# FFN input products by seven block products for eight, in a streaming encoder step on one Trainium2 core

## The reference

```python
D_MODEL, SEQ, DEC_SEQ, D_FF = 1024, 512, 32, 2816

def swiglu(h, w_in, w_out):
    gate, up = jnp.split(h @ w_in, 2, axis=-1)
    return (jax.nn.silu(gate) * up) @ w_out

def encoder_layer(x, l):                     # shortened
    x = x + 0.5 * swiglu(rms_norm(x, ffn1_norm[l]), ffn1_w_in[l], ffn1_w_out[l])
    x = x + mixer(rms_norm(x, mix_norm[l]))
    x = x + 0.5 * swiglu(rms_norm(x, ffn2_norm[l]), ffn2_w_in[l], ffn2_w_out[l])
    return x
```

## Time and profile before

| | us |
|---|---|
| median of 3 runs | 2440.68 |
| lowest and highest | 2438.52 and 2443.16 |
| profiled execution, own time | 2437.53 |
| its span, first to last instruction | 2435.7 |
| TensorE busy | 2394.6 |
| VectorE busy | 1091.7 |
| ScalarE busy | 786.6 |
| GpSimd busy | 375.9 |

### The profile page before, as it was taken

One profiled execution on the slowest core, in us unless ns is written; L12 is line 12 of the kernel. 1 busy time (PEld: TensorE's weight loads), 2 busy tenths in 40 slices (PEclk: granted clock), 3 DMA queues, 4 the chain that ended last, 5 costly groups with the idle time before them and its releaser, 6 DMA issues.

```text
span 2435.7 us, 45344 instructions
## 1 busy us (share of the span) xinstructions
PE 2394.6 (98%) x19160; PEld 2344.4 (96%) x19160; DVE 1091.7 (45%) x1405; ACT 786.6 (32%) x1006; POOL 375.9 (15%) x324
## 2 busy tenths in 40 slices
PE   7999999999999999999999999999999999999998
PEld 7999999988989999999999999999999899999998
DVE  5333332556574333322433332488655654333322
ACT  4333322333323222222322222345345543222222
POOL 2101000000142111000111100143033531011000
PEclk9999999999999999999999999999999999999999
DMA  3223223322202222222222222323200012222221
GB/s 127 91 86 99 82 79 103 101 89 83 68 21 93 87 86 86 82 96 84 95 94 86 86 78 96 98 70 87 71 29 1 10 44 87 87 95 92 83 92 54
DMA packets 191213, 193.66 MB, mean 80 GB/s; under 512 B 4811, under 2 KB 188495, under 8 KB 191082
## 3 DMA queue, kind: packets, MB, share of 16 engines
q1 hardware_dynamic: 178286, 181.64, 23.1%
q10 hardware_dynamic: 12162, 8.11, 1.2%
q0 software_dynamic: 640, 2.10, 0.3%
HBM read 185.73 MB, written 6.10 MB: 79 GB/s over the span
## 4 chain that ended last, share of the span: by engine, by line
PE 94%; DVE 4%; issue 1%; ACT 1%; POOL 0%; DMA 0%; ACTq 0%; DVEq 0%
PE ps L573 81%; PE ps L2522 1%; PE ps L2507 1%; PE ps L2653 1%; DVE wl L558 1%; PE ps L2495 1%; PE ps L1092 0%; PE ps L1560 0%; PE ps L1657 0%; PE ps L780 0%; PE ps L2547 0%; PE ps L2541 0%; PE ps L2553 0%; PE ps L2562 0%; PE ps L1708 0%
## 5 line engine op out<-in xcount | busy, mean ns | idle before, releaser
L573 PE MATMUL ps<-xh,wh 128*128 128x288 f32 x3776 | 780.6, 288 | 3.6 <-DVE wl L558 2.8
L573 PE MATMUL ps<-xl,wh 128*128 128x288 f32 x3776 | 778.4, 287 | 0.0
L573 PE MATMUL ps<-xh,wl 128*128 128x288 f32 x3776 | 775.3, 287 | 0.0
L558 DVE TENSOR_TENSOR wl<-raw,wh 128x2048 fp32r<-128x2048 f32 (+1 forms) x173 | 390.7, 2258 | 505.0 <-ACT wh L553 505.0
L573 PEld LDWEIGHTS ps<-xh,wh 128*128 128x128 f32 x3776 | 577.4, 188 | 16.2 <-issue 8.0
L573 PEld LDWEIGHTS ps<-xh,wl 128*128 128x128 f32 x3776 | 578.1, 188 | 0.0
L573 PEld LDWEIGHTS ps<-xl,wh 128*128 128x128 f32 x3776 | 576.2, 188 | 0.0
L553 ACT ACTIVATE wh<-raw 128x2048 fp32r<-128x2048 f32 (+1 forms) x173 | 323.3, 1869 | 324.7 <-PE ps L573 318.8
L573 PE MATMUL ps<-hl,wh 128*128 128x288 f32 (+1 forms) x1408 | 289.9, 287 | 0.0
L573 PE MATMUL ps<-hh,wl 128*128 128x288 f32 (+1 forms) x1408 | 288.7, 286 | 0.0
L573 PE MATMUL ps<-hh,wh 128*128 128x288 f32 (+1 forms) x1408 | 286.7, 285 | 0.0
(11 more groups left out here) (430 smaller groups left out, 2191.5 us busy)
## 6 DMA issues: line engine op xcount, KB each, us to landing
raw<-ffn_w_in SPq DMA_DIRECT2D x88, 1024.0 KB, 5.1
raw<-ffn_w_out SPq DMA_DIRECT2D x32, 1024.0 KB, 5.1
raw<-odd_w_in SPq DMA_DIRECT2D x16, 1024.0 KB, 5.6
raw<-even_w_in SPq DMA_DIRECT2D x14, 1024.0 KB, 5.0
...
raw<-even_w_out SPq DMA_DIRECT2D x4, 1024.0 KB, 5.3
raw<-odd_w_out SPq DMA_DIRECT2D x4, 1024.0 KB, 5.4
xnat<-x_prompt SPq DMA_DIRECT2D x2, 1024.0 KB, 8.5
```

Source lines behind the costliest of these rows:

```text
L558: nc.vector.tensor_tensor(wl[slot][:, 0:kt, :], raw[slot][:, 0:kt, :], wh[slot][:, 0:kt, :].bitcast(F32), ALU.subtract).then_inc(lo_done.s ...
L573: ins = nc.tensor.matmul(ps[:, 2 * pe_out + b, PCOLS[b]], w, r[:, rk, TOKENS[b]], start=first and a == 0, stop=last and a == 2)
```

## The change

The input matrices. Each FFN keeps three kinds of units:

- the first gate unit, whole as before (96 matmuls);
- the other three units of the first two pairs, "plain": the same 96 matmuls, but the weights split in four blocks of 4 k tiles x 128 columns;
- the 18 units of the other nine pairs, "seven": the unit's weights are seen as 2 x 2 blocks (column tile c by depth half h), the normalised activations as 2 x 2 blocks (depth half by token half of 272 columns, `TH`), and the 2 x 2 x 2 = 8 block products become 7, each 4 k tiles x 3 passes = 12 matmuls of 272 columns into one bank: 84 matmuls. Two products are added onto a bank that holds an earlier one.

For this the activations of an FFN are normalised in full (gain and `rstd`) into `bopf`, POOL forms four block differences of them, and all seven operands are split into high and low (`bop`, 14 blocks). Of each seven unit's weights POOL forms four sums of blocks (`weight_sums`); three of the seven weight operands are raw blocks. ACT and DVE split the seven operands into a ring of eight block entries, which lies in the old `wh` and `wl` buffers. The four output blocks (2 column tiles x 2 token halves) are put together from the banks by ACT (a copy, `m1c`) and DVE (`u2c`, `u3c` and the sums onto them). No `rstd` is needed behind a seven unit, since its input is normalised.

The output matrix. The three weight parts (`HID_PARTS`, 8, 8 and 6 hidden tiles) are no longer an inner loop: after pairs 0 to 3 come four output units over hidden tiles 0 to 7, after pairs 4 to 7 four over tiles 8 to 15, after pairs 8 to 10 four over 16 to 21. `hh` and `hl` shrink to 8 tiles, `x` is added to three times a tile. The matmuls stay 1056. All loops of the FFNs, and those of the mixers' output matrices, are unrolled.

The core of the diff, added lines:

```diff
+    S_ORDER = (6, 2, 3, 1, 4, 0, 5)
+    S_BANK = (0, 1, 2, 3, 0, 1, 2)
+    S_OPEN = (0, 1, 2, 3, 5)
+    S_ADDED = (4, 6)
...
+    def op_split_hi(act, u, i):
+        op, slot = u.op + i, u.raw % 2
+        if i == 0:
+            act.wait_ge(raw_loaded[slot].sem, raw_loaded[slot].at(8 * (u.raw - slot) + 16))
+        if u.kind == "seven" and i in (1, 2, 3, 6):
+            act.wait_ge(sum_made.sem, sum_made.at(4 * u.seven + {1: 2, 2: 2, 3: 3, 6: 4}[i]))
+        if op in op_first:
+            act.wait_ge(unit_done.sem, unit_done.at(op_first[op]))
+        elif op_prev[op] is not None:
+            act.wait_ge(op_used.sem, op_used.at(op_prev[op] + 1))
+        nc.scalar.activation(entry(op)[0][:, 0:block_nk(u, i), :], op_source(u, i), ACT.Copy).then_inc(op_hi.sem, 1)
+
+    def op_split_lo(dve, u, i):
+        op, nk = u.op + i, block_nk(u, i)
+        hi, lo = entry(op)
+        dve.wait_ge(op_hi.sem, op_hi.at(op + 1))
+        nc.vector.tensor_tensor(lo[:, 0:nk, :], op_source(u, i), hi[:, 0:nk, :].bitcast(F32), ALU.subtract).then_inc(op_lo.sem, 1)
+
...
+    def ffn_seven_pe(pe, u, n):
+        f, bank = u.f, 4 * u.s
+        before = ffns[f][u.at - 2]
+        if before.kind == "plain":
+            done = gate_scaled if u.s == 0 else h_made
+            pe.wait_ge(done.sem, done.at((2 * LEAD_PAIRS if u.s == 0 else 2 * FJ) * f + 2 * LEAD_PAIRS))
+        elif before.kind == "out":
+            pe.wait_ge(x_part.sem, x_part.at(16 * f + 8 * before.part + 2 * before.pair + 2))
+        else:
+            pe.wait_ge(block_out.sem, block_out.at(outs_before[before.seven + 1]))
+            if u.s == 0:
+                pe.wait_ge(block_silu.sem, block_silu.at(3 * (before.seven // 2) + 1))
+        for i, o in enumerate(S_ORDER):
+            op = u.op + i
+            pe.wait_ge(op_lo.sem, op_lo.at(op + 1))
+            if u.at == 2 * LEAD_PAIRS:
+                pe.wait_ge(bop_lo.sem, bop_lo.at(7 * f + i + 1))
+            if i == 4:
+                pe.wait_ge(m1_copied.sem, m1_copied.at(u.seven + 1))
+            if i == 5:
+                pe.wait_ge(block_out.sem, block_out.at(outs_before[u.seven] + 1))
+            if i == 6:
+                pe.wait_ge(block_out.sem, block_out.at(outs_before[u.seven] + 3))
+            w_hi, w_lo = entry(op)
+            for k in range(KH):
+                for a, (w, r) in enumerate(((w_hi, 7 + o), (w_hi, o), (w_lo, 7 + o))):
+                    ins = nc.tensor.matmul(ps[:, bank + S_BANK[i], 0:TH], w[:, k, :], bop[:, r, k, :],
+                                           start=i in S_OPEN and k == 0 and a == 0,
+                                           stop=k == KH - 1 and a == 2, skip_group_check=i in S_ADDED)
+            ins.then_inc(op_used.sem, 1)
...
+    def bop_normed(dve, f, n, k):
+
+        first = 6 if k < KH else 4
+        nc.vector.scalar_tensor_tensor(out=bopf[:, first:first + 2, k % KH, :], in0=two(x[:, k, :]), scalar=gain(n, k),
+                                       in1=two(rstd[:]), op0=ALU.mult, op1=ALU.mult).then_inc(bop_norm.sem, 1)
...
+            pool.wait_ge(gate_silu.sem, gate_silu.at(2 * LEAD_PAIRS * f + 2 * j + c + 1))
+            nc.gpsimd.tensor_tensor(gbuf[c][:], gbuf[c][:], rstd[:], ALU.mult).then_inc(gate_rstd.sem, 1)
+
+        def token_sum(out, a, b, done, needs):
+            pool.wait_ge(bop_norm.sem, bop_norm.at(8 * f + done))
+            if needs:
+                pool.wait_ge(bop_sum.sem, bop_sum.at(4 * f + needs))
+            nc.gpsimd.tensor_tensor(bopf[:, out, :, :], bopf[:, a, :, :], bopf[:, b, :, :], ALU.subtract).then_inc(bop_sum.sem, 1)
+
+        gate(0, 0)
+        gate(0, 1)
+        token_sum(3, 7, 6, 4, 0)
+        token_sum(1, 5, 7, 8, 0)
+        token_sum(2, 5, 3, 8, 1)
+        token_sum(0, 4, 2, 8, 3)
+        weight_sums(pool, ffns[f][4])
+        gate(1, 0)
+        gate(1, 1)
...
+    def weight_sums(pool, u):
+
+        s, slot, out = u.seven, u.raw % 2, sums_of(u)
+        first = u.seven - ffns[u.f][2 * LEAD_PAIRS].seven
+        pool.wait_ge(raw_loaded[slot].sem, raw_loaded[slot].at(8 * (u.raw - slot) + 16))
+        if first in (2, 3):
+            pool.wait_ge(op_used.sem, op_used.at(ffns[u.f][2 * LEAD_PAIRS].op))
+        elif first > 3:
+            back = [v for v in ffns[u.f] if v.kind == "seven" and v.seven == s - 2][0]
+            pool.wait_ge(op_lo.sem, op_lo.at(back.op + 7))
+        nc.gpsimd.tensor_tensor(out[:, 0, :, :], block_raw(u, 1, 0), block_raw(u, 1, 1), ALU.add).then_inc(sum_made.sem, 1)
+        pool.wait_ge(sum_made.sem, sum_made.at(4 * s + 1))
+        nc.gpsimd.tensor_tensor(out[:, 1, :, :], out[:, 0, :, :], block_raw(u, 0, 0), ALU.subtract).then_inc(sum_made.sem, 1)
+        nc.gpsimd.tensor_tensor(out[:, 2, :, :], block_raw(u, 0, 0), block_raw(u, 1, 0), ALU.subtract).then_inc(sum_made.sem, 1)
+        pool.wait_ge(sum_made.sem, sum_made.at(4 * s + 2))
+        nc.gpsimd.tensor_tensor(out[:, 3, :, :], block_raw(u, 0, 1), out[:, 1, :, :], ALU.subtract).then_inc(sum_made.sem, 1)
...
+        hidden_lo(dve, units[1], 1, 2)
+        for i in range(4):
+            op_split_lo(dve, units[3], i)
         if f == 0:
             lam_dve(dve)
+        gate(1, 0)
+        for i in range(4):
+            bop_split_lo(dve, f, i)
+        gate(1, 1)
+        op_split_lo(dve, units[4], 0)
+        bop_split_lo(dve, f, 4)
+        op_split_lo(dve, units[4], 1)
+        bop_split_lo(dve, f, 5)
+        hidden(1, 0)
+        op_split_lo(dve, units[4], 2)
+        bop_split_lo(dve, f, 6)
+        for i in (3, 4, 5, 6):
+            op_split_lo(dve, units[4], i)
+        hidden(1, 1)
...
+    def ffn_seven_act(act, u):
+        pair = u.seven // 2
+        tail_act(act, ffns[u.f][u.at - 1])
+        next_split(act, op_split_hi, u, 0)
+        act.wait_ge(op_used.sem, op_used.at(u.op + 1))
+        if u.seven:
+            act.wait_ge(block_out.sem, block_out.at(outs_before[u.seven - 1] + 1))
+        nc.scalar.activation(m1c[:], ps[:, 4 * u.s, 0:TH], ACT.Copy).then_inc(m1_copied.sem, 1)
+        for i in (1, 2, 3, 4):
+            next_split(act, op_split_hi, u, i)
+        if u.s == 0:
+            act.wait_ge(h_made.sem, h_made.at(2 * FJ * u.f + 2 * u.pair))
+            act.wait_ge(op_used.sem, op_used.at(u.op + 5))
+            nc.scalar.activation(gbuf[0][:, 0:TH], ps[:, 4 * u.s, 0:TH], ACT.Silu).then_inc(block_silu.sem, 1)
+        next_split(act, op_split_hi, u, 5)
+        next_split(act, op_split_hi, u, 6)
+        if u.s == 0:
+            act.wait_ge(block_out.sem, block_out.at(outs_before[u.seven] + 4))
+            nc.scalar.activation(gbuf[1][:], gbuf[1][:], ACT.Silu).then_inc(block_silu.sem, 1)
+        else:
+            hidden_hi(act, u, 1, 1)
...
+    def tail_dve(dve, u):
+
+        if u.kind != "seven":
+            return
+        into = gbuf if u.s == 0 else sq
+        dve.wait_ge(op_used.sem, op_used.at(u.op + 7))
+        nc.vector.tensor_tensor(into[0][:, TH:T], u2c[:], ps[:, 4 * u.s + 2, 0:TH], ALU.add).then_inc(block_out.sem, 1)
+        if u.s == 1:
+            dve.wait_ge(block_silu.sem, block_silu.at(3 * (u.seven // 2) + 3))
+            dve.wait_ge(block_out.sem, block_out.at(outs_before[u.seven] + 6))
+            nc.vector.tensor_tensor(sq[0][:, TH:T], sq[0][:, TH:T], gbuf[0][:, TH:T], ALU.mult).then_inc(h_made.sem, 1)
+            hidden_lo(dve, u, 1, 1)
+
+    def late_tail_dve(dve, u):
+
+        if u.kind == "seven" and u.s == 1:
+            hidden_lo(dve, u, 0, 2)
+
+    def ffn_seven_dve(dve, u):
+        before, pair, outs = ffns[u.f][u.at - 1], u.seven // 2, outs_before[u.seven]
+        into = gbuf if u.s == 0 else sq
+        bank = lambda i: ps[:, 4 * u.s + i, 0:TH]
+        tail_dve(dve, before)
+        next_split(dve, op_split_lo, u, 0)
+        late_tail_dve(dve, before)
+        next_split(dve, op_split_lo, u, 1)
+        dve.wait_ge(m1_copied.sem, m1_copied.at(u.seven + 1))
+        dve.wait_ge(op_used.sem, op_used.at(u.op + 2))
+        nc.vector.tensor_tensor(u2c[:], m1c[:], bank(1), ALU.add).then_inc(block_out.sem, 1)
+        next_split(dve, op_split_lo, u, 2)
+        next_split(dve, op_split_lo, u, 3)
+        dve.wait_ge(block_out.sem, block_out.at(outs + 1))
+        dve.wait_ge(op_used.sem, op_used.at(u.op + 4))
+        nc.vector.tensor_tensor(u3c[:], u2c[:], bank(3), ALU.add).then_inc(block_out.sem, 1)
+        dve.wait_ge(block_out.sem, block_out.at(outs + 2))
+        nc.vector.tensor_tensor(into[1][:, TH:T], u3c[:], bank(2), ALU.add).then_inc(block_out.sem, 1)
+        next_split(dve, op_split_lo, u, 4)
+        if u.s == 1:
+            dve.wait_ge(block_silu.sem, block_silu.at(3 * pair + 1))
+            dve.wait_ge(op_used.sem, op_used.at(u.op + 5))
+            nc.vector.tensor_tensor(sq[0][:, 0:TH], bank(0), gbuf[0][:, 0:TH], ALU.mult).then_inc(block_out.sem, 1)
+        next_split(dve, op_split_lo, u, 5)
+        dve.wait_ge(op_used.sem, op_used.at(u.op + 6))
```

(17 more changed lines are left out.)

583 lines of the change are left out of this document (402 added, 181 removed).

## The result

The changed kernel takes **2425.68 us** (median of 4 runs, 2423.9 to 2427.67), the kernel before 2440.4 in the same session: a ratio of **0.9939 [0.9922, 0.9956]**. It is faster, by 15 us. The forecast was 2411, by 30. The profiled execution took 2426.8 us, its span is 2424.5.

What follows compares the result with a forecast made beforehand. PE, busy 98% of the span, was taken as the bound: 94 us saved less 64 of waits, net 30, gave a median of 2411 us. Its own case was 2375 to 2435 (0.45), 2355 to 2470 for 8 in 10.

Steps and rivals of the forecast that it cites:

- (b): Later gate units, one in the third weight part and two in the second: PE waits 5.4 us an FFN.
- The saving: PE's 72 product units of 84 matmuls at 126.0 ns, for 96 at 123.9: 94 us saved.
- (a): From an FFN's start to the end of its first product unit: PE waits 9.3 us an FFN.
- The price of a POOL instruction: DVE loses a POOL instruction's length less 0.40 us: 0.86 a weight sum, 2.1 a difference of 1088.
- (c): From the last product unit to an output unit, 12 times: PE waits 0.3 us each, 3.6 in all.
- late loads: In the first FFN, late loads add a bound of 0 to 4 us, taken as 2.
- Rival 1: DVE and POOL mesh, leaving only the waits before output units: 2340 to 2352 us, chance 0.15.
- Rival 2: One-bank product matmuls of 272 columns cost 133 ns, so the saving is 50 us: 2455, chance 0.07.
- Rival 4: The saving is eaten exactly, within 0.2%, by waits between the two prices; chance 0.08.
- Rival 3: POOL holds DVE for its whole instruction; waits 128 us, half-clock runs some 1.7 us each on top: 2475, chance 0.25.

Runs made afterwards that it cites:

- e8: The changed kernel with POOL's four token differences at each FFN start replaced by memsets that read nothing; 2406.3 us.
- e2: The changed kernel with POOL's four weight sums of each product unit replaced by memsets that read nothing from SBUF; 2364.4 us.
- e5: The changed kernel with the weight sums and the four token differences of each FFN start moved from POOL to DVE; 2394.6 us.
- e10: The changed kernel with POOL's weight sums, from the fifth product unit, held for the third product two units ahead, and token differences on DVE; 2415.2 us.
- e12: The changed kernel with POOL's weight sums, from the fifth product unit, held for the third addition two units ahead, and token differences on DVE; 2401.5 us.

## Why the prediction was right or wrong

**Direction and mechanism: right.** The time fell, by half of what was forecast, and lies in the stated 2375 to 2435. The measured waits are in the two kinds of place that were named, and those of (b) are where they were put: two gate units of the second weight part and one of the third, in each FFN, mostly in front of the seventh product (1.8 to 2.1 us; in three FFNs the second of them only 0.4 to 0.7, and the last of the fourth 1.05).

**The saving: right.** A one-bank product matmul was priced at 126.0 ns from the earlier trace rows; it is 126.2, and the output part has its 123.9 of the earlier trace rows. 94 us stand.

**(a), predicted 9.3 an FFN, measured 11.6** (with the 0.2 by which each stretch reads short). The step was nearly right. In the second FFN PE starts 47.6 before the 812.85 of the chain, at 765.3 (the 0.9 us of its sum of squares left out, as in the prediction); the freeing addition ends at 832.75, t = 67.5, where the sum had 66.0. Where the 1.5 belongs is open. The token difference, priced at 2.5 us from rows at 544 and 2048 elements, takes 3.01; but without its reading DVE's stretch is 7.6 us shorter (e8) and without that of the weight sums 8.1 (e2), where the sum had 8.4 and 8.6 for them. Another 1.1 is lost behind that addition, most of it in the third product unit, with waits at 852.85 and 854.87. PE's own waits in that stretch come to 6.9 us and no more, for the clock was at the lower level for some 10 us of it (granted clock 0.91 on average) and PE arrived late itself. That slowness lay under DVE's lateness.

```profile
812.90:867.20 54.30, 47.36 (x338) 45.94 (x339) 46.18 (x65) 27.79 (x50) 22.28 (x13) 0.91 0.24 78
```

**(b), predicted 5.4 an FFN, measured 8.2** (31.2 and the 1.6 of its zero, over four). PE's recorded waits in the later stretches are 5.0, 7.2, 5.1 and 3.6 us in the four FFNs: 5.2 on average, as predicted. The missing 2.8 is mostly a term that the sum left out. In five of the eight stretches a half-clock run of 3.4 us followed a wait, and these five lose 1.8 to 2.4 us more than they wait; the other three, without one, lose at most 0.5 more. Compare with the stretch at 1338.70 above (granted clock 0.54, 16 matmuls) this one, behind a wait of 2.09 us:

```profile
1477.00:1480.50 3.50, 3.50 (x28) 3.50 (x29) 2.48 (x6) 1.83 (x4) 0.00 (x0) 1.00 0.35 110
```

The prediction had the row for it and the price, 1.7 us, but put it into its third rival instead of into its own sum. Why a wait of 2.09 at 1476.9 was not followed by such a run and one of 1.78 at 1338.75 was, no run here shows.

**The price of a POOL instruction** (its length less 0.40, 0.86 for a weight sum) was too high as an average, 0.52 by DVE's busy time; that part of POOL's reading falls beside sums with PSUM and in DVE's pauses is the likely reason. Where DVE has no pause it was a little too low: 1.0 for each of eight at the start of an FFN. A token difference cost DVE 1.7 (e8) to 2.3 us (e5, e10 and e12, with the 1.28 of DVE's own making added back), priced at 2.1. Where three sums meet the splits ahead of the addition, as in the rows above, DVE lost 3.0 us, 1.0 each: there they had also grown to 1.6 to 1.8 us. So the places that the sum was made for had about the price that it used, which is why the waits of (a) and (b) nearly came out.

**(c), predicted 3.6, measured 0.** Too cautious; what covers it was named.

**The sum.** With the zero put right (a) and (b) are 46.3 + 32.8 = 79.1, and 2.7 more are in the first FFN's plain units (38.4 us against 35.7 in the others). That is 81.8 of losses for the 64 predicted: 18 of the 19 us between 30 and 11. The 2.7 were forecast as 2 for late loads, and that this came near is luck. PE ran at the lower clock there, after and before (length; busy of PE, PEld, DVE, ACT, POOL; granted clock; DMA):

```profile
41.90:48.70 6.80, 6.80 (x29) 6.10 (x29) 6.70 (x10) 4.06 (x5) 2.70 (x2) 0.50 0.02 4
41.90:48.70 6.80, 6.80 (x54) 6.68 (x54) 4.20 (x9) 4.87 (x5) 2.70 (x2) 1.00 0.01 4
```

Another 2 are in the second mixer, from one reciprocal (L716) to the next 475.17 us against 473.18, with no line changed. 1.4 of it is this, before and after (DVE and POOL in each):

```profile
1899.68 3.35 DVE L2009 TENSOR_TENSOR db<-db,ort 128x512 f32<-128x512 f32 x2
1898.33 5.83 POOL L2357 TENSOR_TENSOR dBl<-dBT,dlev 128x512 f32<-128x512 f32 x4
...
1892.59 4.75 DVE L2471 TENSOR_TENSOR db<-db,ort 128x512 f32<-128x512 f32 x2
1891.22 4.97 POOL L2819 TENSOR_TENSOR dBl<-dBT,dlev 128x512 f32<-128x512 f32 x4
```

The same pair of engines met in the same code, and this time DVE lost. In the first mixer 1.5 us were won, where the half clock of the earlier trace rows is gone. Under 1 us of the difference is left over.

**The rivals.** Rival 1 (they mesh) holds in e2 for the later units, once the weight sums read nothing; e2's 2364 is still over the rival's 2340 to 2352, with 13 us left in (a). Rival 2 is refuted by 126.2. Rival 4, a gain eaten within 0.2%, by the interval. Rival 3 (the hold is for the whole instruction) did not come true, but it was nearer than the average of 0.52 looks: in the places where PE waits a weight sum cost 1.0, between the 0.86 of the forecast and the 1.26 of the rival, which put the turning point at 1.05, and its half-clock runs came. Its statement that 23.5 us of losses an FFN eat the gain holds: there were 20.5, and 3 an FFN were gained.
